# Convolution pieces placed around the softmax, a projection unit split ahead, and the entry of two feed-forward blocks summed later

## What is computed

```python
# first block, mixer
q, k, v, gb, gc, xs = split(h @ w_in + b_in)          # 18 units of 128 columns
y_attn = sliding_window_attention(rope(q), rope(k), v, sinks)
y_conv = gc * causal_dwconv3(gb * xs, conv_w)          # the 12 last units, three by three
# second block
h = rwkv7_time_mix(...)                                # ends with (y * g) @ w_o
x = x + rmsnorm(h, g1)
h = swiglu(rmsnorm(x, g2), w_gate, w_up, w_down)       # silu(h @ w_gate) * (h @ w_up), twice in the block
```

## Time and profile before

| | before |
|---|---|
| median of 3 runs | 2073.39 us |
| the profiled execution | 2070.89 us |
| its span | 2069.2 us |
| TensorE (matmul) busy | 1973.0 us, 95% |
| VectorE, ScalarE, GpSimd busy | 1064.3, 777.8, 252.5 us |
| mean granted TensorE clock | 0.968 |

### The profile page before, as it was taken

How to read it: one execution, slowest core, us unless ns; L and a number is a source line. 1 busy time by engine, 2 the same in 40 slices (tenths; PEclk the granted TensorE clock), 3 DMA queues, 4 the chain that set the end, 5 groups by cost and what they waited for, 6 DMA issues and landing times.

```text
span 2069.2 us, 35297 instructions
## 1 busy us (share of the span) xinstructions
PE 1973.0 (95%) x14503; PEld 1577.7 (76%) x14503; DVE 1064.3 (51%) x1567; ACT 777.8 (38%) x1242; POOL 252.5 (12%) x282
## 2 busy tenths in 40 slices
PE   6999899999999999799999999999989999999997
PEld 5767678888886677677777788888867878888886
DVE  6776775455324645687753744442255564444223
ACT  4333433333222335576643423222245443232221
POOL 1100000000014000322311211111100021111110
PEclk8998999999999999899999999999999999999998
DMA  8544323333332132000003133333222223333321
GB/s 309 164 132 122 92 72 93 100 92 112 101 92 73 52 92 85 6 10 7 7 27 102 44 102 98 96 113 97 81 64 79 82 72 102 92 100 100 111 84 41
DMA packets 311057, 181.09 MB, mean 88 GB/s; under 512 B 16381, under 2 KB 303763, under 8 KB 310932
## 3 DMA queue, kind: packets, MB, share of 16 engines
q1 hardware_dynamic: 305506, 162.29, 26.3%
q0 software_dynamic: 4608, 16.78, 2.6%
q10 hardware_dynamic: 818, 0.21, 0.0%
HBM read 177.16 MB, written 2.10 MB: 87 GB/s over the span
## 4 chain that ended last, share of the span: by engine, by line
PE 85%; DVE 8%; ACT 3%; issue 3%; ACTq 1%; POOL 0%; DVEq 0%; POOLq 0%
PE bank L258 22%; PE bank L260 22%; PE bank L259 22%; PE bank L2221 4%; DVE x L1399 1%; PE bank L2734 1%; ACT whi L236 1%; PE bank L1256 1%; PE bank L2728 1%; PE bank L1258 1%; PE bank L1257 1%; PE bank L562 1%; PE bank L2835 1%; DVE wlo L243 1%; PE bank L2006 1%
## 5 line engine op out<-in xcount | busy, mean ns | idle before, releaser
L243 DVE TENSOR_TENSOR wlo<-raw,whi 128x1024 fp32r<-128x1024 f32 (+1 forms) x254 | 331.1, 1304 | 665.3 <-ACT whi L236 665.1
L236 ACT ACTIVATE whi<-raw 128x1024 fp32r<-128x1024 f32 (+1 forms) x254 | 284.1, 1119 | 664.2 <-PE bank L260 657.9
L258 PE MATMUL bank<-fh_hi,whi 128*128 128x512 f32 x991 | 387.7, 391 | 0.9 <-DVE fh_lo L483 0.5
L259 PE MATMUL bank<-fh_lo,whi 128*128 128x512 f32 x991 | 386.3, 390 | 0.0
L260 PE MATMUL bank<-fh_hi,wlo 128*128 128x512 f32 x991 | 386.2, 390 | 0.0
L258 PEld LDWEIGHTS bank<-fh_hi,whi 128*128 128x128 f32 x991 | 186.4, 188 | 42.2 <-DVE fh_lo L483 1.8
L259 PEld LDWEIGHTS bank<-fh_lo,whi 128*128 128x128 f32 x991 | 186.5, 188 | 39.0 <-issue 0.5
L260 PEld LDWEIGHTS bank<-fh_hi,wlo 128*128 128x128 f32 x991 | 186.4, 188 | 38.9
L258 PE MATMUL bank<-f_hi,whi 128*128 128x512 f32 x528 | 205.7, 390 | 0.0
L260 PE MATMUL bank<-f_hi,wlo 128*128 128x512 f32 x528 | 205.4, 389 | 0.0
L259 PE MATMUL bank<-f_lo,whi 128*128 128x512 f32 x528 | 205.4, 389 | 0.0
(11 more groups left out here) (478 smaller groups left out, 3223.8 us busy)
## 6 DMA issues: line engine op xcount, KB each, us to landing
raw<-in_w_up_dram SPq DMA_DIRECT2D x44, 512.0 KB, 3.7
raw<-in_ffn_w_gate_dram SPq DMA_DIRECT2D x44, 512.0 KB, 3.7
raw<-in_ffn_w_up_dram SPq DMA_DIRECT2D x44, 512.0 KB, 3.7
raw<-in_ffn_w_down_dram SPq DMA_DIRECT2D x32, 704.0 KB, 4.2
late<-in_ada_w_dram POOLq DMA_DIRECT2D x32, 512.0 KB, 4.1
raw<-in_rwkv_w_rkv_dram SPq DMA_DIRECT2D x24, 512.0 KB, 3.4
raw<-in_w_down_dram SPq DMA_DIRECT2D x16, 704.0 KB, 4.2
early<-in_ada_w_dram SPq DMA_DIRECT2D x16, 512.0 KB, 14.2
```

The costliest lines, as they stand in the source:

```text
L236: act.activation(halves_of(at)[0][:, 0:kts * P], raw_unit(at, kts), ACT.Copy).then_inc(hi_ready, 1)
L243: dve.tensor_tensor(lo[:, 0:kts * P], raw_unit(at, kts), hi[:, 0:kts * P].bitcast(F32), ALU.subtract)\
L258: pe.matmul(dst, hi, rhs_hi(k), start=first and k == 0, stop=False)
L259: pe.matmul(dst, hi, rhs_lo(k), start=False, stop=False)
```

## The change

Three edits. **In the mixer** four tiles of unit 6 are done before attention starts, and the other 92 are dealt as 5 or 6 per step, so that a unit no longer ends just at the end of a step; the convolution is cut into product, taps and gate, placed in front of, between and behind the parts of the softmax; a split whose unit ends within a step's last two tiles goes behind part a. **In the time mix's projection** unit 2 gets memory of its own (`w_third`) and is split in the last round; the units behind it are split into the slots of units 1 and 0. **At the entry of the two feed-forward parts** the squares go to eight slots of their own, GpSimd adds them all up (seven adds) when the last is there, the sum on TensorE is moved behind units 4 and 5, the splits of units 6 and 7 are moved in front of root and reciprocal, and VectorE adds to x with the plain form (L1395).

```diff
+    class LateNorm(Norm):
+        def pool_sum(self, pool):
+            wait(pool, sum_step.sem, self.sum0)
+            pool.wait_ge(sq_ready.sem, self.sq0 + self.n)
+            for k in range(1, self.n):
+                self.pool_add(pool, k)
+        def pe_sums(self, pe):
+            wait(pe, std_ready.sem, self.std0)
+            pe.wait_ge(acc_step.sem, self.acc0 + self.n - 1)
+            pe.matmul(bank[NORM_BANK][:, :], ones[:, :], sq_sum[:, :], start=True, stop=True).then_inc(sum_step.sem, 1)
...
             elif part < 2:
-                pe.wait_ge(prj_ready, N_PRE)
+                pe.wait_ge(prj_ready, N_PRE - 1 + part)
...
-    KS = (N_IN - N_PRE) * KD // len(STEPS)
+    AHEAD = 4
+    def step_start(i):
+        return AHEAD + ((N_IN - N_PRE) * KD - AHEAD) * i // len(STEPS)
+    def ends_late(i, u):
+        return step_start(i + 1) - (u + 1 - N_PRE) * KD < 2
...
+        pe_in(pe, N_PRE, range(AHEAD))
         pe_rotate(pe, N_PRE - 1)
         pe_scores(pe, 0)
...
         for i in range(len(STEPS)):
+            j, softmax = conv_of(i), i + 1 < len(STEPS)
+            if j is not None:
+                conv_product(dve, j)
             for u in ended(i):
-                dve_in(dve, u)
-            if i + 1 < len(STEPS):
+                if not (softmax and ends_late(i, u)):
+                    dve_in(dve, u)
+            if softmax:
                 dve_softmax_a(dve, i + 1)
+            for u in ended(i):
+                if softmax and ends_late(i, u):
+                    dve_in(dve, u)
+            if j is not None:
+                conv_tap(dve, j, 0)
+                conv_tap(dve, j, 1)
+            if softmax:
                 dve_softmax_b(dve, i + 1)
+            if j is not None:
+                conv_tap(dve, j, 2)
+                conv_gate(dve, j)
             ada_accumulate(dve, LATE_STEP[i])
...
+                    in_sq = sbs(part, f"in_sq{tag}", [P, KD, T])
...
-                    self.norm.pe_sums(pe)
                     return
...
                     if b[1] == NORM_BANK:
-                        pe.wait_ge(std_ready.sem, self.norm.std0 + 1)
+                        self.norm.pe_sums(pe)
+                        for g in range(2):
+                            if g:
+                                pe.wait_ge(std_ready.sem, self.norm.std0 + 1)
+                            unit_products(pe, self.at_up(i, 2 * q + g), KD, bank[b[g]][:, :], hi, lo, True, True)
+                        continue
...
                 for n in range(2):
                     split_hi(act, self.at_up(1, n), free=self.at0.plus(-1))
+                for n in range(2, 4):
+                    split_hi(act, self.at_up(1, n))
                 self.norm.act_root(act)
...
-                if i == 0:
-                    split_hi(act, self.at_up(1, 2 + q))
...
-                self.lead.dve(dve, self.lead.res.add_beside_pool)
-                for n in range(2):
+                self.lead.dve(dve)
+                for n in range(4):
                     split_lo(dve, self.at_up(1, n))
                 self.norm.dve_rstd(dve)
...
-                    elif p < 2:
-                        split_lo(dve, self.at_up(1, 2 + q))
...
+                if j == KD - 1:
+                    act.wait_ge(ys_ready, KD // 2)
+                    split_hi(act, out_tm.units[2], free=out_tm.at0.plus(-1))
...
+        def splits_at(self, o):
+            if self.early and o < 2:
+                return self.units[o + 3], self.units[1 - o]
+            if self.early and o == 2 or o >= KD - 2:
+                return None
+            return self.units[o + 2], self.units[o]
         def act(self, act):
             for o in range(KD):
-                at = self.at0.plus(o)
-                if o < KD - 2:
-                    split_hi(act, at.plus(2))
-                else:
+                at = self.units[o]
+                if self.splits_at(o):
+                    nxt, free = self.splits_at(o)
+                    split_hi(act, nxt, free=free)
```

More of the change, by code:

```diff
@@ new lines, in conv_product, with conv_tap @@
+    def conv_product(dve, j):
+        dve.wait_ge(unit_done, at_in[N_PRE + 3 * j + 2].count)
+        dve.wait_ge(gb_ready, j + 1)
+        wait(dve, conv_done, j - 1)
+        if j == 0:
+            dve.wait_ge(rope_done, 5)
+        dve.scalar_tensor_tensor(cbuf[:, j % 2, 2:T + 2], bank[MIX[2]][:, :], v("b_in", 10 + j), gb_sb[:, j % 2, :],
+                                 ALU.add, ALU.mult).then_inc(conv_p, 1)
+    def conv_tap(dve, j, w):
+        c, acc = cbuf[:, j % 2, :], cacc[:, j % 2, :]
+        if w == 0:
+            dve.wait_ge(conv_p, j + 1)
+            dve.tensor_scalar(acc, c[:, 0:T], v("conv_w", j), None, ALU.mult).then_inc(conv_t, 1)
+        else:
+            dve.wait_ge(conv_t, 3 * j + w)
+            dve.scalar_tensor_tensor(acc, c[:, w:T + w], v("conv_w", 4 * w + j), acc, ALU.mult, ALU.add)\
+               .then_inc(conv_t, 1)
@@ L1059, in pe_rotate, with conv_gate @@
+    def conv_gate(dve, j):
+        dve.wait_ge(conv_t, 3 * j + 3)
+        dve.scalar_tensor_tensor(y_cv[:, j, :], bank[MIX[1]][:, :], v("b_in", 6 + j), cacc[:, j % 2, :],
+                                 ALU.add, ALU.mult).then_inc(conv_done, 1)
     def pe_rotate(pe, u):
@@ L1198, in ended, with conv_of @@
         return [u for u, ks in pieces(i) if ks[-1] == KD - 1]
+    def ends_late(i, u):
+        return step_start(i + 1) - (u + 1 - N_PRE) * KD < 2
+    def conv_of(i):
+        return next(((u - N_PRE) // 3 for u in ended(i) if (u - N_PRE) % 3 == 2), None)
     def pe_mixer1(pe):
@@ L1442, in __init__ @@
             self.f_hi = sbs(mem, f"f_hi{tag}", [P, KF, T], F32R)
+            if not conv:
+                with ExitStack() as part:
+                    sbs(part, f"f_low2{tag}", [P, 2, T], F32R)
+                    in_sq = sbs(part, f"in_sq{tag}", [P, KD, T])
             self.f_lo = sbs(mem, f"f_lo{tag}", [P, KF, T], F32R)
@@ L1460, in __init__ @@
             else:
-                self.norm = Norm(x_tile, KD, before.ready)
+                self.norm = LateNorm(x_tile, KD, before.ready,
+                                     [in_sq[:, k, :] for k in range(KD)])
                 self.lead = Lead(before, gains, hi, lo, self.norm)
@@ L2653, in body @@
                 dve_state(dve, j, 7)
+                if j == KD - 1:
+                    split_lo(dve, out_tm.units[2])
             if inv:
@@ L3103, in __init__ @@
             self.end = at0.plus(KD)
+            self.units = [at0.plus(o) for o in range(KD)]
+            if early:
+                self.units[2].held = w_third[:, 0, :], w_third[:, 1, :]
             self.o = mem
@@ L3160, in pe @@
                 if o < KD - 1:
-                    unit_products(pe, self.at0.plus(o), KD, bank[o % 2][:, :], hi, lo, True, True)
+                    unit_products(pe, self.units[o], KD, bank[o % 2][:, :], hi, lo, True, True)
             for ks in (range(KD - 1), range(KD - 1, KD)):
```

41 lines of the change are left out of this document (16 added, 25 removed).

## The result

The changed kernel takes 2076.58 us (median of 20 runs) against 2072.40 us of the kernel before (20 runs, the same chip): a ratio of 1.0023, 95% interval 1.0012 to 1.0033. That is 4.2 us more (2.5 to 6.8 by the interval): within 0.3%, as forecast (2075 us), and on the slower side of no change. The profiled execution of after has a span of 2076.2 us, and 7.0 us more than that of before.

The account below looks back on a forecast made before the run. TensorE was taken as the bound, holding 85% of the chain of waits. Mixer -18.2, projection -0.2 and entries 2 x (7.6 + 2.2) give +1.2 on 2070.9, so 2072.1; with 2.5 for the median, 2075 us, range 2066 to 2084.

Parts of the forecast that it names:

- The mixer, -18.2: Attention steps: TensorE restarts behind the last convolution at 196.8 instead of 214.90 us, 18.2 us less; bounds 22.5 and 14.
- the five stalls summing to 2.35 us: Attention steps: TensorE stalled by 0.3, 0.45, 0.5, 1.0 and 0.1 us as VectorE's part a runs behind its scores.
- The walk of VectorE's queue: Attention steps: VectorE's work summed from 93.9 to 189.8 us, so VectorE, not TensorE at 185.6, sets the steps' end.
- next to no idle time of VectorE between 110 and 190 us: Sign in the mixer that the forecast is right: VectorE has next to no idle time there after the change.
- this wait of 1.25 us: Attention steps: VectorE's wait for the exponentials inside its 5.30 us period, now holding a late split or taps 0 and 1.
- The tail of the mixer: Behind the mixer's restart: the sum carried the whole 18.2 us gain to the end, with no clock loss there.
- rival (b): Longer half clock: 5.1 us lost per entry, up to 2.9 more at the steps' end; 2083 us, chance 0.19.
- The projection, -0.2: Projection: unit 2 waits for the copy of bank 0 behind unit 3's split, starting at 1098.7 instead of 1098.89.
- The entries, +7.6 each: Both feed-forward entries: TensorE arrives 2.1 us earlier but waits 10.2 us before unit 8, net 7.6 us later each.
- Rival (a): Entries don't stall: root and pairs are hidden, TensorE keeps 2.1 us each; total -22.6, 2051 us, chance 0.08.
- The clock, +2.2 each: Entries: half clock behind the 10 us wait costs 2.2 us each, taken between 0 and 5.1.
- The sum: Whole kernel: -18.2 - 0.2 + 2 x (7.6 + 2.2) = +1.2 us against the profiled 2070.9, so 2072.1.

Follow-up runs that it names:

- mix_only: The kernel before with only the mixer's edits; 2055.11 us, ratio 0.9926 to before.
- entry_free: After with splits of units 8 and 9 inside pairs 0 and 1, units 8 to 11 waiting only for the pair whose banks they take; 2068.82 us.
- best: entry_free with, in the projection, ScalarE's copy of bank 0 ahead of the split of unit 3; 2067.58 us, ratio 0.9983 to before.
- splits_early: After with only the splits of units 8 and 9 moved into pairs 0 and 1; 2077.18 us, ratio 1.0023 to before.
- sum_early: After with the norm's sum between units 4 and 5, the root ahead of unit 7's split, that split within pair 0; 2067.94 us.
- four_early: entry_free with the splits of units 10 and 11 also moved, into pairs 2 and 3; 2052.55 us, ratio 0.9912 to before.
- all_four: After with copy first, sum early, splits of units 7 to 11 in pairs 0 to 4, eased waits of units 8 to 11; 2055.74 us.
- pool_at_once: After with GpSimd adding each square as soon as it is there; 2076.71 us, ratio 1.0023 to before.

## Why the prediction was right

**The mixer, -18.2.** Measured -19.3 at the restart in the profiled execution (18.7 in mix_only; over the nine traces with the whole of the mixer's edits the restart lies between 195.4 and 198.5, so 16.4 to 19.5 us earlier). The terms held: the last gate at 192.83 against 194.0, the restart 2.75 us later as today; half-clock stretches at 88, 126, 153 and 187 us are gone. Of the five stalls summing to 2.35 us there were, in the trace of after, 1.9 us in three waits for probabilities and one of 0.3 us for `y_cv` that I had not seen: tile 0 of unit 10 goes to a bank that the first convolution's gate still reads. The walk of VectorE's queue was 1.2 us too long, and one sign that it named was wrong: there should be next to no idle time of VectorE between 110 and 190 us. The stretch (columns as above) has 67.06 of 80 us busy; below it VectorE's own waits in the same stretch, and the last matmul of unit 17.

```profile
110.00:190.00 80.00, 78.20 (x424) 59.32 (x422) 67.06 (x163) 33.51 (x97) 6.87 (x13) 1.00 0.49 145
...
DVE st L1166 <- ACT st L1157: 11.1, 9, 1.3
...
186.99 0.39 PE L260 MATMUL bank<-h_hi,wlo 128*128 128x512 f32 x1
```

The sign was badly drawn, not the mechanism. All that VectorE waits for in these 80 us is ScalarE's exponentials, nine times up to 1.3 us, and the walk had counted this wait of 1.25 us inside every period of 5.30. It never waits for TensorE. Unit 17 ends at some 187.4 us and its product runs at 188.94, behind other work of VectorE without a pause. So VectorE's queue with the exponentials in it does set the end of the steps, but by 1.6 us and not by the 4.2 of the prediction (185.6 against 189.8); TensorE, busy for 78.20 of the 80 us at full clock, is almost as tight.

**The tail of the mixer was mis-sized.** I let the gain arrive whole at the end. Behind the restart the clock stays at half for 6.80 us instead of 3.4, up to 201.20, and in some executions once more at 225; 0.6 to 4.2 us of the gain are lost up to the end of this group in after and the runs with the mixer's edits (19.3 to 16.6 in after, 18.7 to 15.9 in mix_only, 19.4 to 18.7 in entry_free, 18.6 to 14.4 in best). This was in rival (b) as "as much as 2.9 more at the end of the steps", and belonged into the sum.

**The projection, -0.2.** The wait has the name and the size that the prediction gave it: the copy, not the split, 1.69 us for 1.95. best shows the other reading of the row: with the copy ahead there is no wait at all, but 1.7 us are nothing that this kernel's times can show.

**The entries, +7.6 each.** From the entry's first product to unit 8 after takes 1181.56 - 1124.6 = 56.96 us, before 1187.66 - 1138.5 = 49.16: +7.8. The wait was 9.86 for 10.2, the pair 4.74 for 4.75, and what TensorE won ahead of it 1.8 for 2.1. That the split of unit 8 and not a bank set it was right by 2.9 us; the prediction didn't look at the other condition, pair 2's product, which for the forecast made no difference and for a repair does: with both splits moved into the pairs the product is the last, and 1.0 us is all that is gained (splits_early). Rival (a), that the chain is hidden, was wrong; GpSimd's adds ended at 1151.4, well ahead, as said.

**The clock, +2.2 each.** The entries cost 10.4 and 10.5 us, so 2.6 and 2.7 beyond the 7.8. The half clock ends 6.1 us after the restart; the value of 2.2 was chosen between 0 and 5.1 without a row that fixes it, so that it came out within 0.5 us is in part luck. Over the 20 runs of after the mean granted clock is 0.9656, over the 23 and 35 runs of before beside the experiments 0.9677 to 0.9683. That is no measure of this term: the mean also counts the stretches that went in the mixer and the half clock over TensorE's idle time. In time, sum_early and entry_free took little from the clock: their waits of 5.4 and 5.7 us still bring half clock behind them (6.8 us long at the first entry in both), and only without such waits (four_early, all_four) is there none between 1124 and 1485. The Trainium skill, "TensorE: Matmul & The Clock Gate", section "Why this matters for your kernels", says that a long idle gap puts the clock back to half, and it does here, behind 9.9, 5.7 and 5.4 us; behind 1.89 us in four_early it doesn't.

**The sum.** -19.3 - 0.3 + 20.9 = +1.3 against +1.2 forecast; measured +7.0 between the two profiled executions and +4.2 in the medians. What is left of the 7.0 lies in the 2.7 us behind the mixer (less the 1.4 won back in front of the first entry beyond the projection's own 0.3), and in the recurrence, 4.4: a stretch at half clock of 13.7 us at 1013.5 in after, against three of 3.4 us at 873, 901 and 1027 in before. That isn't the change's. Up to the entries splits_early is the same program as after, and in its profiled execution the same stretch reads

```profile
1013.50:1027.30 13.80, 13.68 (x401) 11.63 (x398) 10.62 (x29) 9.24 (x27) 2.68 (x4) 1.00 0.01 4
```

with 401 matmuls instead of 228. Six executions with the same program up to the entries reach the first entry at 1118.8 us (four_early), 1121.9 (splits_early), 1122.6 (entry_free), 1124.6 (after), 1124.8 (pool_at_once) and 1126.9 (sum_early): a spread of 8 us. It goes with the clock: up to there the earliest had 61 us at half clock, the latest 79.

So the difference of two terms near 19 us came out right because each of them held within 2 us. But the forecast change was +1.2 and the measured one +4.2. Of the 3 us, by the parts' medians, some 1.1 are the mixer (-17.1 for -18.2, the tail) and 1.8 the entries (+21.4 for +19.6, the clock in the main); each is less than its interval. That 2075 lies nearer to 2076.58 than this is luck: it holds 2.5 us for the distance from the profiled execution of before to the median of 3 runs, and over 20 runs that distance is 1.5.

## What to carry to other kernels

When work is moved in a chain that ends in a tie with the bounding engine, lay out the chain as it will stand: what is removed (here 7 x 1.1 us of VectorE, worth 1 us to TensorE) counts for little against one element of the chain that moves behind 10.9 us of products. Where such a wait appears, look at every condition of the waiting instruction and at the next two or three of the same kind behind it: of 9.9 us one edit took 1.0, two took 4.1, four splits with the eased waits took 8.0, and only all of them took it whole. Work that is moved into an earlier place also makes that place longer (here 1.0 us for each split within a pair). And before trusting a few microseconds between two profiled executions, compare their stretches of clock.

## What the runs showed of the hardware

The clock granted to TensorE fell to half in the recurrence of after at 1013.5 us and stayed there for 13.7 us, in which TensorE was busy throughout. In the 6.8 us ahead of the fall it had been busy for 5.59 us, its longest wait near it 1.2 us. In splits_early, the same program up to there, it was busy for 5.58 us of the same 6.8, and the clock stayed at full; why it fell in the one and not in the other, these runs don't tell. The clock goes with most of a kernel's spread: over the 20 runs of after granted clock and time are correlated at -0.91, from 2071.2 us to 2085.8.

VectorE's split of 128x1024 takes 1.23 us alone. Two of them took 3.69 us beside GpSimd's adds in after and 2.36 us in the same place of before, where GpSimd stood still; one took 1.40 us beside GpSimd's product in a pair. Work of VectorE that is put into a gap in which GpSimd reads is not free.
